# Branch B attention: scores from high and low halves of the queries stacked on the contraction, against split keys, with one pass for the window masks

## The reference

```python
q, k, v = project(p_lat, True)          # rotary on q and k
qc, kc, vc = project(p_ctx, False)
...
s_loc = jnp.where(valid, jnp.einsum('bhgnqd,bhnkd->bhgnqk', qb, kb).astype(jnp.float32) * scale, NEG_INF)
s_ctx = jnp.einsum('bhgnqd,bhcd->bhgnqc', qb, kc).astype(jnp.float32) * scale
...
pr = jax.nn.softmax(jnp.concatenate([s_ctx, s_loc, s_sink], axis=-1), axis=-1)
o = (jnp.einsum('bhgnqc,bhcd->bhgnqd', pr[..., :n_ctx], vc)
     + jnp.einsum('bhgnqk,bhnkd->bhgnqd', pr[..., n_ctx:n_ctx + 3 * Q_BLOCK], vb))
```

## Time and profile before

| | |
|---|---|
| median of 3 runs | 3343.31 us (3334.99 to 3349.95) |
| profiled execution, its own time | 3357.3 us |
| its span, first to last instruction | 3355.6 us |
| TensorE busy with matmuls | 3134.9 us, 93% |
| VectorE, ScalarE, GpSimd busy | 42%, 35%, 5% |
| mean granted TensorE clock | 0.964 |

### The profile page before, as it was taken

The page is one execution under the profiler, slowest core; times in us unless marked ns, Lnnn a source line. Parts: engine busy times, 40 slices in busy tenths (PEclk is TensorE's granted clock), DMA queues, the critical chain, the costliest instruction groups (busy, mean ns, idle before and its releaser), DMA issues.

```text
span 3355.6 us, 39886 instructions
## 1 busy us (share of the span) xinstructions
PE 3134.9 (93%) x16256; PEld 2418.2 (72%) x16256; DVE 1414.6 (42%) x2288; ACT 1167.2 (35%) x2019; POOL 165.6 (5%) x179
## 2 busy tenths in 40 slices
PE   6988899999999999899999989888999999889998
PEld 4877785577667768788888867777456567578887
DVE  4266742333443435423232332774333444454444
ACT  4343333333443343412121234443332443442222
POOL 0023300000000000000000000320000000000000
PEclk8999998999999999999999989999997999999999
DMA  5222240031103123233333322223021021323332
GB/s 186 75 84 79 81 135 25 19 106 62 52 27 113 59 92 102 78 105 101 101 106 102 95 82 60 85 76 126 7 80 47 13 89 48 107 76 100 94 99 90
DMA packets 83759, 273.82 MB, mean 82 GB/s; under 512 B 9344, under 2 KB 9600, under 8 KB 82688
## 3 DMA queue, kind: packets, MB, share of 16 engines
q1 hardware_dynamic: 74896, 229.84, 21.7%
q0 software_dynamic: 8688, 41.49, 3.7%
HBM read 245.07 MB, written 26.21 MB: 81 GB/s over the span
## 4 chain that ended last, share of the span: by engine, by line
PE 87%; ACT 5%; DVE 5%; issue 2%; DMA 2%; SPq 0%; DVEq 0%; ACTq 0%
PE slot L615 84%; PE slot L1019 2%; DMA raw<-w_merge_dram 1%; ACT tmp L1209 1%; DVE wl L1517 1%; ACT PT_B L1392 0%; ACT Hh L1211 0%; DMA SS<-g_kept 0%; ACT wh L1118 0%; DVE XS L1783 0%; ACT Yh L1386 0%; ACT logits_out L1161 0%; DVE XS L1722 0%; DMA X<-xT_dram 0%; DMA g_kept<-logits_out 0%
## 5 line engine op out<-in xcount | busy, mean ns | idle before, releaser
L615 PE MATMUL slot<-Hh,wh 128*128 128x512 f32 (+1 forms) x2368 | 885.9, 375 | 48.4 <-DVE Hl L1564 15.1
L615 PE MATMUL slot<-Hl,wh 128*128 128x512 f32 (+1 forms) x2368 | 843.2, 357 | 0.0
L615 PE MATMUL slot<-Hh,wl 128*128 128x512 f32 (+1 forms) x2368 | 841.9, 357 | 0.0
L615 PEld LDWEIGHTS slot<-Hh,wh 128*128 128x128 f32 x2368 | 455.4, 193 | 166.4 <-issue 77.7
L615 PEld LDWEIGHTS slot<-Hh,wl 128*128 128x128 f32 x2368 | 455.2, 193 | 64.9
L615 PEld LDWEIGHTS slot<-Hl,wh 128*128 128x128 f32 x2368 | 456.3, 193 | 61.1 <-issue 5.8
L1517 DVE TENSOR_TENSOR wl<-raw,wh 128x1024 fp32r<-128x1024 f32 (+1 forms) x208 | 228.5, 1099 | 232.5 <-ACT wh L1118 229.5
L1841 DVE TENSOR_REDUCE rowmax<-slot 128x1 f32<-128x768 f32 (+3 forms) x160 | 123.4, 771 | 412.6 <-PE slot L615 412.0
L615 PE MATMUL slot<-Uh,wh 128*128 128x512 f32 (+1 forms) x768 | 274.3, 357 | 0.0
L615 PE MATMUL slot<-Ul,wh 128*128 128x512 f32 (+1 forms) x768 | 272.0, 354 | 0.0
L615 PE MATMUL slot<-Uh,wl 128*128 128x512 f32 (+1 forms) x768 | 271.5, 354 | 0.0
(11 more groups left out here) (229 smaller groups left out, 4099.8 us busy)
## 6 DMA issues: line engine op xcount, KB each, us to landing
raw<-w_dram SPq DMA_DIRECT2D x204, 512.0 KB, 3.6
raw<-w_gate_dram SPq DMA_DIRECT2D x64, 512.0 KB, 3.6
ada_g_raw<-ada_dram POOLq DMA_DIRECT2D x48, 512.0 KB, 3.9
ada_g_raw<-ada_dram SPq DMA_DIRECT2D x32, 512.0 KB, 3.9
raw<-w_merge_dram SPq DMA_DIRECT2D x64, 256.0 KB, 2.7
g_kept<-logits_out SPq DMA_DIRECT2D x32, 384.0 KB, 2.3
SS<-g_kept SPq DMA_DIRECT2D x32, 384.0 KB, 3.3
ada_first<-ada_dram SPq DMA_DIRECT2D x8, 1024.0 KB, 18.2
```

The lines of the kernel that those rows point to most:

```text
L615: return pe.matmul(dst, lhsT, rhs, start=start, stop=stop)
```

## The change

The scores are no longer computed from fp32 operands. After its rotation each query head of 64 features is split into a high part (fp32r) and the rest, and both are laid over each other in one tile of 128 partitions (`QS`): for group 0 the high part in partitions 0 to 63 and the rest in 64 to 127, for group 1 the other way round. The keys of each group are split likewise, and each half is written twice, into partitions 0 to 63 and 64 to 127 (`K_HIGH[g]`, `K_LOW[g]`). One product of `QS` with `K_HIGH` and one with `K_LOW` give all four terms. The near keys of a tile are contiguous, so both products run over all of them at once; the masks are added by one fp32r product each, from fp32r copies of the identity and the masks, which are laid over the cosine table. Splits are made by ScalarE (`split_into_high`) and VectorE (`split_into_low`) during the projection, two steps behind the job. The key job moves to the head of B's list, and so does its weight tile. A projected tile now goes through three rotating buffers (`QT`); ScalarE's third and fourth query copies wait for a buffer's split.

```diff
-    "B": [("q", j) for j in range(4)] + [("k", 0), ("v", 0)],
+    "B": [("k", 0)] + [("q", j) for j in range(4)] + [("v", 0)],
...
+        ident_r, winmask_r = at("ident_r", [P], f32r, tab_offset), at("winmask_r", [2, P], f32r, tab_offset + P * 4)
...
-        QB, KB = XS[:, 1:5, :], XS[:, 0, :]
+        QS = rows("QS", R_X, B_HEADS, f32r)
+        KS = [rows(f"KS{k}", R_S + k, 1, f32r) for k in range(3)] + [rows("KS3", R_S + 12, 1, f32r)]
+        K_HIGH, K_LOW = [KS[0][:, 0, :], KS[1][:, 0, :]], [KS[2][:, 0, :], KS[3][:, 0, :]]
+        QT = [SS[:, 3 + k, :] for k in range(3)]
...
TensorE, attention
-                            q = QB[part, j, qs_]
-                            for x, m in enumerate(tile["keys"][:tile["lat"]]):
-                                dst = out_s[:, a + x * P:a + (x + 1) * P]
-                                edge = m != n
-                                mm(dst, q, KB[part, m * P:(m + 1) * P], start=True, stop=not edge)
-                                if edge:
-                                    mm(dst, ident[:, :], winmask[:, 0 if m < n else 1, :], start=False, stop=True)
-                            last = mm(out_s[:, SEQ:T], q, KB[part, SEQ:T])
+                            q = QS[:, 2 * j + g, qs_]
+                            near = tile["keys"][:tile["lat"]]
+                            edges = [m for m in near if m != n]
+                            if near:
+                                keys = slice(near[0] * P, (near[-1] + 1) * P)
+                                mm(out_s[:, a:SEQ], q, K_HIGH[g][:, keys], start=True, stop=False)
+                                mm(out_s[:, a:SEQ], q, K_LOW[g][:, keys], start=False, stop=False)
+                            for m in edges:
+                                dst = out_s[:, a + (m - near[0]) * P:a + (m - near[0] + 1) * P]
+                                mm(dst, ident_r[:, :], winmask_r[:, 0 if m < n else 1, :], start=False, stop=m == edges[-1])
+                            mm(out_s[:, SEQ:T], q, K_HIGH[g][:, SEQ:T], start=True, stop=False)
+                            last = mm(out_s[:, SEQ:T], q, K_LOW[g][:, SEQ:T], start=False, stop=True)
TensorE, ahead of it
-                    if b == "B" and layer == 0:
-                        pe.wait_ge(masks_in.sem, w.next(masks_in, 2))
+                    if b == "B":
+                        pe.wait_ge(split_low.sem, w.next(split_low, B_SPLITS))
+                        pe.wait_ge(masks_split.sem, w.next(masks_split))
ScalarE, project
+                        if n >= 3:
+                            act.wait_ge(split_low.sem, w.next(split_low))
-                        act.activation(QB[:, j, 0:nn] if kind == "q" else KB[:, 0:nn], s[:, 0:nn], ACT.Copy).then_inc(copied.sem, 1)
+                        act.activation(rotated("B", kind, j)[:, 0:nn], s[:, 0:nn], ACT.Copy).then_inc(copied.sem, 1)
...
+                def split_into_high(kind, j):
+                    act.wait_ge(roped.sem, w.next(roped))
+                    src = rotated("B", kind, j)
+                    for g in range(B_KV):
+                        part = slice(g * B_HD, (g + 1) * B_HD)
+                        if kind == "q":
+                            ins = act.activation(QS[part, 2 * j + g, 0:nq], src[part, 0:nq], ACT.Copy)
+                        else:
+                            for copy in range(2):
+                                ins = act.activation(K_HIGH[g][copy * B_HD:(copy + 1) * B_HD, 0:T], src[part, 0:T], ACT.Copy)
+                    ins.then_inc(split_high.sem, 1)
...
+                    if branch == "B" and n >= 2 and plan[n - 2][0] in "qk":
+                        split_into_high(*plan[n - 2])
...
+                    act.activation(ident_r[:, :], ident, ACT.Copy)
+                    act.activation(winmask_r[:, :, :], winmask[:, :, :], ACT.Copy).then_inc(masks_split.sem, 1)
+                    act.wait_ge(split_low.sem, w.next(split_low, B_SPLITS - 2))
VectorE, project, behind rope
+                    if branch == "B" and n >= 2 and plan[n - 2][0] in "qk":
+                        split_into_low(nq, *plan[n - 2])
...
+            def split_into_low(nq, kind, j):
+                dve.wait_ge(split_high.sem, w.next(split_high))
+                src = rotated("B", kind, j)
+                for g in range(B_KV):
+                    part, other = slice(g * B_HD, (g + 1) * B_HD), slice((1 - g) * B_HD, (2 - g) * B_HD)
+                    if kind == "q":
+                        high = QS[part, 2 * j + g, 0:nq].bitcast(f32)
+                        ins = dve.tensor_tensor(QS[other, 2 * j + g, 0:nq], src[part, 0:nq], high, ALU.subtract)
+                    else:
+                        high = K_HIGH[g][part, 0:T].bitcast(f32)
+                        for copy in range(2):
+                            ins = dve.tensor_tensor(K_LOW[g][copy * B_HD:(copy + 1) * B_HD, 0:T], src[part, 0:T], high, ALU.subtract)
+                ins.then_inc(split_low.sem, 1)
```

More of the change, by code:

```diff
@@ L230, in build @@
         cursor = [offset]
+        const_at = {}
         def const(name, shape):
+            const_at[name] = cursor[0]
             t = at(name, shape, f32, cursor[0])
@@ L252, in build @@
         nsink = const("nsink", [B_HEADS])
+        tab_offset = const_at["tab"]
+        ident_r, winmask_r = at("ident_r", [P], f32r, tab_offset), at("winmask_r", [2, P], f32r, tab_offset + P * 4)
         cos_t, sin_t, rot_t = tab[:, 0:SEQ], tab[:, SEQ:2 * SEQ], tab[:, 2 * SEQ:2 * SEQ + P]
@@ L273, in build @@
         masks_in = sig("masks_in", unit=16)
+        split_high, split_low, masks_split = sig("split_high"), sig("split_low"), sig("masks_split")
         ada_g_full = [sig(f"ada_g_full{k}", unit=16) for k in range(2)]
@@ L336, in build @@
         COPIES = {b: sum({"r": 0, "v": 2}.get(kind, 1) for kind, _ in PROJ[b]) for b in BRANCHES}
+        B_SPLITS = sum(kind != "v" for kind, _ in PROJ["B"])
         COPIES["A"] += A_HEADS + A_HEADS // 2 + A_HEADS + NB
@@ L437, in build @@
         RSTD = {"A": [XS[:, 5, :], XS[:, 6, :]], "D": [SS[:, 2, :], SS[:, 3, :]]}
-        ROT = {"A": SS[:, 10, :], "B": SS[:, 11, :], "D": SS[:, 11, :]}
+        ROT = {"A": SS[:, 10, :], "B": SS[:, 7, :], "D": SS[:, 11, :]}
         def rotated(branch, kind, j):
             if branch == "B":
-                return QB[:, j, :] if kind == "q" else KB
+                return QT[(1 + j if kind == "q" else 0) % 3]
             return QY[:, j, :] if kind == "q" else KD[:, j, :]
@@ L969, in attention @@
                             g, j = tile["g"], tile["j"]
-                            part = slice(g * B_HD, (g + 1) * B_HD)
-                            q = QB[part, j, qs_]
-                            for x, m in enumerate(tile["keys"][:tile["lat"]]):
-                                dst = out_s[:, a + x * P:a + (x + 1) * P]
-                                edge = m != n
-                                mm(dst, q, KB[part, m * P:(m + 1) * P], start=True, stop=not edge)
-                                if edge:
-                                    mm(dst, ident[:, :], winmask[:, 0 if m < n else 1, :], start=False, stop=True)
-                            last = mm(out_s[:, SEQ:T], q, KB[part, SEQ:T])
+                            q = QS[:, 2 * j + g, qs_]
[10 more added lines that the diff above has]
+                            last = mm(out_s[:, SEQ:T], q, K_LOW[g][:, SEQ:T], start=False, stop=True)
                         else:
@@ L1250, in copy_out @@
                         act.activation(QY[:, j, 0:nn] if kind == "q" else KD[:, j, 0:nn], s[:, 0:nn], ACT.Copy).then_inc(copied.sem, 1)
+                def split_into_high(kind, j):
[9 more added lines that the diff above has]
+                    ins.then_inc(split_high.sem, 1)
+                if branch == "B":
+                    act.wait_ge(roped.sem, w.next(roped, 4 + (6 if layer else 0)))
                 if branch == "C":
@@ L1276, in project @@
                         rsqrt(slot[beside], nq if kind == "q" else T, D_HD, RSTD["D"][(n - 1) % 2])
+                if branch == "B":
+                    if layer == 0:
+                        act.wait_ge(masks_in.sem, w.next(masks_in, 2))
+                    act.activation(ident_r[:, :], ident, ACT.Copy)
+                    act.activation(winmask_r[:, :, :], winmask[:, :, :], ACT.Copy).then_inc(masks_split.sem, 1)
+                    act.wait_ge(split_low.sem, w.next(split_low, B_SPLITS - 2))
                 if branch == "A":
@@ L2057 @@
         heads = [g * B_GROUP + j for j in range(B_GROUP) for g in range(B_KV)]
+        w8.append(tiles_of(w_in[l], span(B0 + B_HEADS * B_HD, B_KV * B_HD)))
         w8.append(tiles_of(w_in[l], np.concatenate([span(B0 + h * B_HD, B_HD) for h in heads])))
-        w8.append(tiles_of(w_in[l], span(B0 + B_HEADS * B_HD, 2 * B_KV * B_HD)))
+        w8.append(tiles_of(w_in[l], span(B0 + (B_HEADS + B_KV) * B_HD, B_KV * B_HD)))
         w8.append(tiles_of(w_in[l], span(D0, (D_HEADS + 2 * D_KV) * D_HD)))
```

4 lines of the change are left out of this document (2 added, 2 removed).

## The result

The changed kernel takes **3249.54 us** in the median of four runs (3245.3 to 3254.4). The kernel before, beside it, takes 3339.15 (four runs, 3328.05 to 3349.95). The ratio is **0.9732**, 95% interval 0.9696 to 0.9768: faster by 2.7%. Forecast: 3265, range 3238 to 3302. The profiled execution has a span of 3243.6 us and took 3245.3.

A forecast was written before the change was run, and what follows sets the result against it. TensorE was taken as the bound in both attentions. The terms -49.7 - 55.2 - 10.5 + 7 + 7 + 2 + 2 + 19 gave -78.4 us, from the median 3343.3 to about 3265 us, range 3238 to 3302.

The forecast's parts named there:

- Scores: Score products in both attentions: cheaper as single fp32r instructions, 49.7 us saved in layer 0, 55.2 in layer 1.
- that moves from the gate's first matmul to the score's first and cancels: In attention tiles: about 0.1 us extra for the first matmul behind fp32 work, taken as no net change.
- The clock: Both attentions: 10.5 us saved on layer 1's other half-clock work, +7 us for new falls after longer pauses.
- The level fell behind the pause: Layer 1: clock fell at the pause ahead of attention, returning only with the first long values product; 48 us at half.
- Tail and key split: Projection: last query splits delay the scores, +7 us; next weight's wait, +2; key split delays layer 1's job 4, +2.
- The wait for the next weight behind the first tiles: Layer 1's attention start: tile 2's scores wait for the next weight's preparation queued behind the last splits, 2 us.
- The chain beside it: Attention: faster TensorE waits on ScalarE and VectorE, mostly at gate tiles; +19 us, ends 8 and 45.
- the chain as the bound: Rival, attention: the ScalarE and VectorE chain takes 45 us instead of 19; 3291 to 3303 us, chance 0.14.
- clock low until the values product: Rival, both attentions: half clock lasts until the first values product, +32 us instead of +7; 3290 us, chance 0.13.
- no cheaper passes: Rival, scores: an fp32r pass costs as much as an fp32 instruction; about 20 us gained, 3323 us, chance 0.03.
- slower than before: Rival: half clock through the whole of both attentions, +171 us and 9 of tail; about 3520 us, chance 0.04.

The follow-up runs named there:

- before again: The kernel before the change, unchanged, profiled in a second execution: 3332.11 us (one run).
- old products: The earlier kernel's blockwise fp32 score products and masks, but from stacked queries and `K_HIGH` (128 rows), low keys left out: 3277.7 us, 0.9826 of before.
- full rows in fp32: The changed kernel with the same score products and masks, all operands read as fp32: 3342.55 us, 1.0013 of before.
- logits first: The changed kernel with ScalarE's copies of the gate logits put ahead of its other copies in the attention stages: 3235.8 us, 0.9702 of before.
- one pass with 64 rows: The changed kernel without the `K_LOW` products and with plain 64-row halves of queries and keys: 3289.38 us, 0.9859 of before.
- early splits: The changed kernel with each split done ahead of the next job's work and VectorE waiting for each half alone: 3254.82 us, 0.9735 of before.

## Why the forecast was right, and where its terms were not

The forecast was -78.4 us; between the medians it is -89.6, in the stages against before again -84.8.

Two sums of the prediction are off, and neither moves the forecast. TensorE's idle time in the earlier trace rows is 5.0 + 5.2 = 10.2 us, not 7.6. By the gaps that it takes from the Trainium skill ("TensorE: Matmul & The Clock Gate", Back-to-back issue gap), an estimate of the scores comes to 40 us, not 43.

**Scores: mis-sized, 93 forecast at full clock, 105 measured.** TensorE's busy time in both attentions fell from 383.3 us (before again) to 275.5; less 3 for the clock, that is 105. The durations between start and start were near: 0.89, 0.67 and 0.32 against 0.86, 0.61 and 0.24. What failed is the sentence "that moves from the gate's first matmul to the score's first and cancels". It doesn't move, it goes: the gate's first matmul is 0.11 shorter and four transposes 0.16. An edge tile so saves 1.28 us, a middle tile 1.90, a context tile 0.57; 16 x (1.28 + 1.90 + 0.57) = 60.0 in layer 0, 16 x 3.18 = 50.9 in layer 1, an estimate from three tiles that comes out 6 us above the busy time. At full clock I had 49.7 and 43.6 (16 x 4.20 = 67.2 in layer 1, less 23.6).

**The reason was half right.** I took the old price for that of fp32 instructions. By the kernels in between, 128 rows with the old products give 56 us, a second pass over the keys in fp32 takes them back (65 between old products and full rows in fp32), and fp32r gives 93 (3342.55 to 3249.54). The stacking that doubles the work of each product also removes the change between 64 and 128 rows, 50 us in the one test and 56 in the other.

**The clock: 12 us too large.** "The level fell behind the pause" read one execution as the kernel, and the saving was then taken off the median, which was 14 us below that execution. Layer 1's slow 48 us gave 11.6 us extra in the scores (78.8 less 67.2) and the 10.5 of the other work, 22 together, of which before again had 12. After, a fall of 6.8 us came in each layer, as forecast, and 10.2 us in layer 1 that were not; TensorE was busy in 18.3 of all, so they cost 9. The forecast was 22 - 7 = 15 gained, the runs show 3.

**Tail and key split:** +11 forecast, +7.1 measured (from the table to the first scores 90.5 to 94.3 and 70.5 to 73.9 against before again). The pauses grew from 1.4 and 1.3 us to 5.2 and 4.1, for the last `QS`, 6.6 of it. So at most 0.6 is left for the key split in layer 1, forecast at 2: TensorE waits 2.0 us for a weight's low part there, and did so in before again. The wait for the next weight behind the first tiles, forecast at 2, isn't in the view.

**The chain beside it:** +19 forecast, +15.9 measured (TensorE's idle time in both attentions, 12.2 us in before again, 28.1 after; 15.6 of it in the waits listed above). Its place was right in layer 0 (the logits' copies) and layer 1 (`PT_B`); logits first shows that 8.2 us of layer 0's waits were only an order in ScalarE's queue.

Put together for the stages: -105.0 - 2.8 + 7.1 + 15.9 = -84.8. The mechanism held, a TensorE bound with cheaper scores. That the total came so near is luck: two errors offset each other, the scores' gain 12 us too small and the clock's 12 us too large. Of the rivals, the chain as the bound (+45), clock low until the values product (6.8 us was all at the start), no cheaper passes and slower than before are out.

## What to carry to other kernels

Cost a matmul by what stands beside it: from the step ahead of it to the step behind it, not by its own slot, above all where the number of rows changes. Don't price a stretch at half clock from a single execution; take a second profile, and look at the mean granted clock of all executions for how often it comes. When one engine gets faster, look at the order in the next engine's queue first: moving one copy was worth more here than two reworked waits.

## What the runs showed of the hardware

- Weights aren't loaded behind the matmul ahead where 64 rows and 128 rows meet. The kernel with 64 rows took some 0.37 us more a tile, with two to four such meetings, in fp32r, beside the clock; the loads of before at 870.38 and 871.00 show the same in fp32.
- With 128 rows, fp32 matmuls of 128 columns follow each other in 0.11 us for each of their two instructions, as fp32r ones do; fp32r gains nothing for one instruction there, but needs one for a product where fp32 needs two. For 384 columns it is 0.33 (2592.03 to 2593.33 for four) against about 0.2.
- fp32r passes of 128 columns take 0.11 us when several follow each other, 0.06 once between passes of 256. Passes of 256 take 0.12 in a stream of gate matmuls and 0.15 in a score tile (2541.09 to 2541.38 for two).
- The same kernel, in the same place, was at half clock for 47.8 us in one execution and 13.7 in another. The mean granted clock was at or under 0.967 in 12 of 42 executions of before and in all four of one pass with 64 rows. In the kernels with 128 rows it was 0.968 or more in 54 executions; the four of early splits had 0.944 once and 0.970 to 0.974 otherwise.
